# Rebuilt expert routing: last output product by column halves, router straight into tokens by experts, earlier normalising, shorter softmax

## The chip, the core and the metric

The kernel runs on one core of a Trainium2 chip. Its engines are TensorE (PE, matrix products; its weight loads are listed apart as PEld), VectorE (DVE), ScalarE (ACT), GpSimd (POOL) and SyncE (SP), which here only issues DMA transfers. Each engine works through a queue of its own in program order; semaphores order them against each other. Products are written to PSUM, eight banks of 128 partitions by 512 float32. The metric is the device time of one execution in microseconds.

## What is computed

Two layers of a diffusion backbone over 128 prompt and 256 sample tokens of width 1024, all in float32. A layer mixes tokens (three branches, gates, one output projection), adds the result to x, normalises and runs a mixture of 16 experts in which each expert chooses its tokens. The capacity is 16 tokens of the prompt and 32 of the samples. The part that matters here, cut from the reference:

```python
def block(x, mod, lp, ctx=None):
    sh1, sc1, g1, sh2, sc2, g2 = jnp.split(mod, N_MOD, axis=-1)
    h = rmsnorm(x, lp['norm1_g']) * (1 + sc1) + sh1
    y, new = token_mixing(h, lp, ctx)
    x = x + g1 * y
    h = rmsnorm(x, lp['norm2_g']) * (1 + sc2) + sh2
    x = x + g2 * ec_moe(h, lp['w_router'], lp['w_gate'], lp['w_up'], lp['w_down'])
    return x, new

def ec_moe(h, w_router, w_gate, w_up, w_down):
    b, n, d = h.shape
    cap = CAPACITY_FACTOR * n // N_EXPERTS
    aff = jax.nn.softmax(jnp.einsum('bnd,de->ben', h, w_router).astype(jnp.float32), axis=1)
    vals, idx = lax.top_k(aff, cap)
    xg = jax.vmap(lambda hb, ib: hb[ib])(h, idx)
    ...
```

## The kernel before

**Tiles and streams.** The 384 tokens are three tiles of 128: tile 0 is the prompt, tiles 1 and 2 the samples, and they are handled in the order 1, 2, 0. Everything is written by hand: each engine's program is a list of steps, and `plan_banks` gives each step its PSUM bank and its turn in it. `wait_full` waits until a bank's product is complete, `wait_read` until it has been read.

**Weights.** They stream from HBM through a ring of eight 1 MB slots (`ring`), in the expert phase sixteen (eight more in `M`, as 2 MB pairs). SyncE issues the loads in one order; each waits until its slot's last reader is done. In a layer the expert stage is eight pairs of experts with twelve 2 MB loads each. Some of the first pair's weights are loaded during mixing. After them come the slots of the last mixing units, which wait for the output products (`wo`), the load that waits for x (`x_mixed`), and the resident weights of the last pair (`load_resident`, into `arena`, `const` and `hT`), which wait for the router of tile 0 and the gate rows. Every later load waits for a product of an expert pair: the first of them for the first half product of the first pair (`first_half_used`).

**Between mixing and experts.** `project_out(n, t, lo, hi)` is the output product of column half n (512 columns) and tile t, eight products (kb) of merged by w_out, of which a call does lo to hi. VectorE's `add_mixed(n, t)` multiplies it by the gate row and adds it to x; the first half signals `x_front`, the second `x_mixed`. TensorE's `turn_x(t, h)` transposes four 128-column blocks of x, and ScalarE or VectorE (`turned`) copies them to `hT`. The router (`router`) then multiplies: its weights `wrA` (32 columns for each block) are the stationary operand, the 128 tokens move, four blocks stand side by side in the array's column groups and leave four partial sums of experts by tokens; ScalarE copies these (`router_part`), and `route` folds and turns them into tokens by experts with one more product. VectorE's `logits` scales by rstd and adds a constant, takes the maximum, subtracts it; ScalarE takes exp; `affinities` sums, inverts and scales. The affinities are turned to experts by tokens (`turn_affinities`), `top` runs rounds of MAX8 and MATCH_REPLACE8 (four for the samples, two for the prompt), `number` numbers the chosen tokens, `turn_slots` turns them back, `slots` copies and `chosen` compares them with slot numbers into the selection `gsel`. The gathers, products of the normalised x (`xn`, by ScalarE's `normal_x`) with gsel write the first group's tokens, which ScalarE and VectorE move to `xcur` (`first_samples`, `first_prompts`). `gate_row` products (L2027) make the rows of the second gate. `merged` lies in the same memory as `xn`, as blocks by all tokens, so that normalising waits for the last output product. Then come the expert pairs (`pair_step`, L2136).

In the trace a float32 product stands as two passes, so `x8` in the program's order is `x16` in the trace; transposes are single.

Of the kernel before, what the change touches and what calls it, by code (L numbers as in the profile page):

```python
# [12 lines left out]
P = 128  # L13
# [30 lines left out]
_sizes = [("ident", P), ("fold", NE), ("slotno", 2 * SLOTS),  # L44
# [11 lines left out]
def const_table():  # L56
# [13 lines left out]
    put("fold", (r[:, None] % 32 == np.arange(NE)[None, :]))  # L70
# [47 lines left out]
def plan_banks(l):  # L118
# [62 lines left out]
    for name, b in ((("wo", 0, 1), 5), (("wo", 1, 1), 6), (("wo", 0, 2), 7), (("xt", 1, 0), 0), (("xt", 1, 1), 1),  # L181
                    (("wo", 1, 2), 5), (("rpart", 1), 2), (("xt", 2, 0), 0), (("route", 1), 3), (("wo", 0, 0), 6),
                    (("xt", 2, 1), 1), (("rpart", 2), 2), (("route", 2), 3), (("wo", 1, 0), 7), (("afft", 0), 4),
                    (("xt", 0, 0), 5), (("slt", 0), 4), (("modb", 10, 0), 6), (("xt", 0, 1), 5), (("modb", 11, 0), 7),
                    (("rpart", 0), 4), (("route", 0), 5), (("afft", 1), 5), (("slt", 1), 5)):
        use(name, b)
# [78 lines left out]
def hybrid_step(nc, a, outs):  # L265
    with ExitStack() as ctx:
# [10 lines left out]
        merged = xn[:, :, :].rearrange("p t d -> p (t d)").rearrange("p (k n) -> p k n", n=TOK)  # L277
# [82 lines left out]
        rpart = arena[:, 1792:2048].rearrange("p (a b) -> p a b", b=P)  # L360
# [22 lines left out]
        fold = cst_("fold")  # L383
# [60 lines left out]
        x_front = sem("x_front")  # L444
        wshift_ready = sem("wshift_ready")
# [87 lines left out]
        def _(sp):  # L533
# [47 lines left out]
            def load_resident(l):  # L581
# [68 lines left out]
        def _(pool):  # L650
# [11 lines left out]
            for l in range(L):  # L662
# [57 lines left out]
                wait_full(pool, l, ("rpart", TILES[-1]))  # L720
# [23 lines left out]
        def _(act):  # L744
# [84 lines left out]
            for l in range(L):  # L829
# [146 lines left out]
                def router_part(t):  # L976

                    ps = wait_full(act, l, ("rpart", t))
                    read(l, ("rpart", t), F(rpart[:, t % 2, :], ps[:, 0:P], ACT.Copy))
# [6 lines left out]
                def normal_x(t):  # L986

                    act.wait_ge(rstd_ready, NPOW * (l + 1) - T + TURN[t] + 1)
                    F(xn[:, t, :], x[:, t, :], ACT.Copy, scale=rstd[:, 95 + t:96 + t]).then_inc(xn2_ready, 1)

                square_x(1)
                turned(1, 0)
                router_part(1)
# [3 lines left out]
                router_part(2)  # L997
                expert_exp(2)
                act.wait_ge(xss_ready, xs[0])
                turned(0, 0)  # L1000
                wait_full(act, l, ("wo", 1, 0))
                normal_x(1)
                square_x(0)
                turned(0, 1)
                router_part(0)
                normal_x(2)
                expert_exp(0)
                normal_x(0)
                for i in (10, 11):
                    ps = wait_full(act, l, ("modb", i, 0))  # L1010
                    if i == 10:
                        wait_full(act, l, ("modb", 11, 0))
                    read(l, ("modb", i, 0), F(g2slot[:, (i - 10) * 512:(i - 9) * 512], ps[:, :], ACT.Copy))
# [51 lines left out]
                first_samples(0)  # L1065
                first_samples(2)
                first_prompts(0)
# [5 lines left out]
        def _(dve):  # L1073
# [92 lines left out]
            def merge(l, b, j):  # L1166
# [3 lines left out]
                dst = merged[:, j, :] if b == 0 else gated  # L1170
                V.scalar_tensor_tensor(dst, tanh_g[:, j % 2, :], 1.0, ps[:, 0:TOK], ALU.add, ALU.mult)\
                    .then_inc(bank_read[turn(l, ("br", b, j))[0]], 1)
                wait_read(dve, l, ("br", b, j))
                if b:
                    V.tensor_tensor(merged[:, j, :], merged[:, j, :], gated, ALU.add).then_inc(merged_ready, 1)
# [1120 lines left out]
```

## Time and profile before

| what | us |
|---|---|
| median of 3 runs (lowest, highest) | 1750.67 (1750.56, 1751.0) |
| the profiled execution, its span | 1750.49, 1748.5 |
| TensorE busy, of the span | 1674.4 (96%) |
| VectorE, ScalarE, GpSimd busy | 659.4, 310.2, 118.7 |
| DMA mean over the span | 306 GB/s |
| output products start, layer 0 and 1 | 381.3, 1247.2 |
| first expert pair starts, layer 0 and 1 | 439.8, 1305.65 |

The rows further on give times in microseconds from the start of the span. A chain of work is read from its end back: each piece is what released the next one or stood ahead of it on its engine. "issue" in it is time in which nothing that the profile shows was waited for. The granted TensorE clock was 1.0 over the whole span, that is 2.4 GHz.

### The profile page before, as it was taken

The page shows a single profiled execution, that of the slowest core. Times are in us where ns is not written, and L with a number is a line of the kernel's source. Part 1 is how long each engine was busy: PE and PEld are TensorE (multiplying, and loading weights), DVE is VectorE, ACT ScalarE, POOL GpSimd, SP SyncE. Part 2 cuts the span into 40 slices and gives each one's busy share as a digit, 9 for nine tenths or more (in the row PEclk, how much of TensorE's full clock was granted, in tenths as well). Part 3 has the DMA queues.
Part 4 walks back from the last instruction along what each step waited for, and adds up shares of the span by engine and source line. Part 5 has one row for each costly group of instructions (what it writes and reads, how often), then busy time and mean ns, then how long its engine had stood idle before and what let it go on. Part 6 is the DMA issues. An engine that isn't in the chain of part 4 may idle for free.

```text
span 1748.5 us, 18810 instructions
## 1 busy us (share of the span) xinstructions
PE 1674.4 (96%) x7072; PEld 782.8 (45%) x7072; DVE 659.4 (38%) x1394; ACT 310.2 (18%) x792; POOL 118.7 (7%) x161
## 2 busy tenths in 40 slices
PE   7999999999999998898999999999999999988988
PEld 3456566554333232242345566665553433323322
DVE  2257666676112120121124566666651111211211
ACT  2234322032001010000022432222130100000100
POOL 0251000000000000000012500000000000000000
PEclk9999999999999999999999999999999999999999
DMA  9531333766999999999983223338669999999997
GB/s 395 191 123 36 134 121 133 294 253 265 383 427 428 427 430 427 430 427 428 426 358 144 103 84 137 117 118 340 258 229 418 426 429 426 430 427 430 428 428 318
DMA packets 51123, 534.33 MB, mean 306 GB/s; under 512 B 6065, under 2 KB 7249, under 8 KB 11377
## 3 DMA queue, kind: packets, MB, share of 16 engines
q1 hardware_dynamic: 47232, 523.27, 72.7%
q0 software_dynamic: 2112, 7.97, 1.3%
q10 hardware_dynamic: 1712, 2.20, 0.4%
q8 instruction: 42, 0.69, 0.2%
q14 instruction: 25, 0.20, 0.0%
HBM read 531.29 MB, written 2.13 MB: 305 GB/s over the span
## 4 chain that ended last, share of the span: by engine, by line
PE 79%; DMA 20%; DVE 1%; issue 0%; POOL 0%; ACT 0%; SPq 0%; DVEq 0%
PE bank L2136 24%; DMA ring<-in_w_moe 18%; PE bank L1722 14%; PE bank L1741 7%; PE bank L1788 6%; PE bank L2173 5%; PE bank L1973 5%; PE bank L1825 2%; DMA ring<-in_w_mix 2%; PE bank L1885 2%; PE bank L2040 1%; PE bank L1750 1%; PE bank L1860 1%; PE bank L1765 1%; PE bank L1710 1%; PE bank L1713 1%
## 5 line engine op out<-in xcount | busy, mean ns | idle before, releaser
L1722 PE MATMUL bank<-hT,ring 128*128 128x384 f32 x768 | 257.7, 489 | 0.0
L2136 PE MATMUL bank<-M,hT 128*64 128x512 f32 x1024 | 227.9, 595 | 16.1 <-DMA M<-in_w_moe 16.1
L2136 PE MATMUL bank<-ring,hT 128*64 128x512 f32 x976 | 220.1, 594 | 9.9 <-DMA ring<-in_w_moe 9.9
L1722 PEld LDWEIGHTS bank<-hT,ring 128*128 128x128 f32 x768 | 142.9, 190 | 99.8 <-issue 8.1
L2136 PEld LDWEIGHTS bank<-M,hT 128*64 128x64 f32 x1024 | 71.6, 137 | 162.7 <-issue 135.0
L2136 PEld LDWEIGHTS bank<-ring,hT 128*64 128x64 f32 x976 | 70.0, 137 | 146.8 <-issue 130.5
L1741 PE MATMUL bank<-M,ring 128*128 128x384 f32 x384 | 132.1, 487 | 0.0
L2136 PE MATMUL bank<-M 128*64 128x512 f32 x512 | 115.4, 595 | 12.9 <-DMA M<-in_w_moe 12.9
L2136 PE MATMUL bank<-ring,M 128*64 128x512 f32 x512 | 115.3, 596 | 12.3 <-DMA ring<-in_w_moe 10.9
L1033 ACT ACTIVATE M<-bank 128x512 f32<-128x512 f32 x32 | 19.1, 598 | 568.2 <-PE bank L2136 568.2
L1788 PE MATMUL bank<-ring,hT 128*128 128x512 f32 (+1 forms) x288 | 117.3, 567 | 1.6 <-DVE hT L1158 1.1
L1602 DVE SCALAR_TENSOR_TENSOR M<-M,bank 128x512 f32<-128x512 f32 x32 | 22.0, 688 | 226.9 <-ACT M L1033 226.9
L1607 DVE SCALAR_TENSOR_TENSOR M<-M,bank 128x512 f32<-128x512 f32 x32 | 22.0, 688 | 209.8 <-PE bank L2136 209.8
L1615 DVE TENSOR_TENSOR M<-bank,g2slot 128x512 f32<-128x512 f32 x32 | 22.1, 692 | 204.0 <-PE bank L2136 204.0
L2173 PE MATMUL bank<-M 128*128 128x512 f32 x192 | 93.7, 622 | 2.5 <-DVE M L1615 2.5
L1741 PEld LDWEIGHTS bank<-M,ring 128*128 128x128 f32 x384 | 71.4, 190 | 47.4 <-ACT M L827 1.1
L1973 PE MATMUL bank<-ring,xn 128*128 128x512 f32 x192 | 86.0, 596 | 0.0
L1403 DVE SCALAR_TENSOR_TENSOR g2slot<-ring,cs,g2slot 128x512 f32<-128x512 f32 x120 | 81.9, 746 | 1.4 <-DVE g2slot L1403 0.4
L1788 PEld LDWEIGHTS bank<-ring,hT 128*128 128x128 f32 x288 | 54.2, 190 | 62.5 <-issue 60.6
L1403 DVE SCALAR_TENSOR_TENSOR arena<-ring,cs,arena 128x512 f32<-128x512 f32 x120 | 81.5, 746 | 0.3
L1626 DVE TENSOR_TENSOR x<-x,bank 128x512 f32<-128x512 f32 x96 | 66.0, 687 | 31.4 <-PE bank L2173 31.4
L2136 PEld LDWEIGHTS bank<-M 128*64 128x64 f32 x512 | 37.0, 137 | 83.9 <-issue 75.4
(249 smaller groups left out, 1547.3 us busy)
## 6 DMA issues: line engine op xcount, KB each, us to landing
ring<-in_w_moe SPq DMA_DIRECT2D x92, 2048.0 KB, 28.6
M<-in_w_moe SPq DMA_DIRECT2D x90, 2048.0 KB, 29.2
ring<-in_w_mix SPq DMA_DIRECT2D x110, 1024.0 KB, 4.9
M<-in_w_moe SPq DMA_DIRECT2D x12, 1024.0 KB, 10.0
arena<-in_w_moe SPq DMA_DIRECT2D x4, 1024.0 KB, 11.7
ring<-in_w_mix SPq DMA_DIRECT2D x4, 576.0 KB, 5.0
arena<-in_bias_rows POOLq DMA_DIRECT2D x4, 512.0 KB, 5.8
g2slot<-in_bias_rows POOLq DMA_DIRECT2D x4, 512.0 KB, 7.3
```

The costliest lines, as they stand in the source:

```text
L1403: ins = V.scalar_tensor_tensor(acc, w[:, q, :], cs[:, kb, s:s + 1], acc, ALU.mult, ALU.add)
L1602: V.scalar_tensor_tensor(th[:, h, :], th[:, h, :], 1.0, bank[b][:, :], ALU.add, ALU.mult)\
L1615: V.tensor_tensor(osb[:, n * 512:(n + 1) * 512], bank[b][:, :], g2slot[:, n * 512:(n + 1) * 512], ALU.mult).then_inc(bank_read[b], 1)
L1626: V.tensor_tensor(xs, xs, bank[b][:, :], ALU.add).then_inc(bank_read[b], 1)
L1722: ins = mm(ps[:, 0:TOK], w[:, q, (j % 4) * P:(j % 4 + 1) * P], hT[:, 4 * h + q, :], start=(h == 0 and q == 0), stop=(h == 1 and q == 3))
L1741: ins = mm(ps[:, 0:TOK], w[:, q, (j % 4) * P:(j % 4 + 1) * P], y[:, q, :], start=(q == 0), stop=(q == 3))
L1788: ins = mm(ps[:, 0:n], hT[:, 4 * h + q, t * P:(t + 1) * P], w[:, q, 0:n], start=(h == 0 and q == 0), stop=(h == 1 and q == 3))
L1825: ins = mm(ps[:, 0:TOK], w[:, q, g * P:(g + 1) * P], hT[:, 4 * h + q, :], start=(h == 0 and q == 0), stop=(h == 1 and q == 3))
L1885: ins = mm(ps[:, :], ckvT[:, k, t * P:(t + 1) * P], w[:, k, h * 512:(h + 1) * 512], start=(k == 0), stop=(k == 1))
L1973: ins = mm(ps[:, :], merged[:, kb, t * P:(t + 1) * P], w[:, kb % 4, :], start=(kb == 0), stop=(kb == 7))
L2136: ins = mm(bank[b][64 * e:64 * e + 64, :], lhs(e, 4 * h + q), w, start=(h == 0 and q == 0), stop=(h == 1 and q == 3))
L2173: mm(bank[b][:, :], selT[:, t * P:(t + 1) * P], osb[:, n * 512:(n + 1) * 512], start=True, stop=True).then_inc(bank_full[b], 1)
```

## The change

It rewrites the stretch between the output products and the first expert pair, in seven places.

- `merged` is stored by tiles, so that each tile's part can be overwritten when its own products are done; `normal_x(1)` and `normal_x(2)` come earlier on ScalarE.
- The router keeps the token block of `hT` (128 columns) as the stationary operand and moves `wrA` (16 columns), which gives tokens by experts at once: `rpart`, `route`, `fold` and ScalarE's copy go. A tile's router is eight products in two calls of four.
- The last output product, of tile 0's second 512 columns, is made as two products of 256 columns (`project_half`), with adds (`add_half`) and turns (`turn_quarter`, `turned_quarter`) of their own; ScalarE squares x(0) in two parts.
- The router's weights are negated, so that the minimum of the negated logits serves ScalarE's exp as its bias, with the sum taken by ScalarE's accumulator.
- VectorE does `top` and `number` of the samples ahead of `add_mixed(0, 0)`.
- The prompt's selection is compared straight out of PSUM over 16 slots of four experts (`chosen_prompt`); GpSimd zeroes the rest once.
- The order of gathers, gate rows and turns on TensorE is another, and `load_resident` also waits for the last rstd.

The diff, cut to its core:

```diff
-        merged = xn[:, :, :].rearrange("p t d -> p (t d)").rearrange("p (k n) -> p k n", n=TOK)
+        merged = xn[:, :, :].rearrange("p t (k c) -> p t k c", c=P)
...
                 wait_full(sp, l, ("modb", 11, 0))
+                sp.wait_ge(rstd_ready, NPOW * (l + 1))
...
+                pool.wait_ge(merged_ready, 24 * (l + 1))
+                nc.gpsimd.memset(gsel[:, 0, :], 0.0).then_inc(gsel_zero, 1)
...
                 def expert_exp(t):
 
                     act.wait_ge(exp_in_ready, 3 * l + TURN[t] + 1)
-                    F(aff[:, t, :], logit[:, t, :], ACT.Exp).then_inc(exp_ready, 1)
+                    F(aff[:, t, :], logit[:, t, :], ACT.Exp, scale=-1.0, bias=small[:, t, 0:1], accum_out=small[:, t, 1:2])\
+                        .then_inc(exp_ready, 1)
...
+                def add_half(h):
+
+                    name = ("wo", 1, 0) if h else ("wo_first", 0)
+                    ps = wait_full(dve, l, name)
+                    lo, hi = 512 + 256 * h, 768 + 256 * h
+                    step(V.tensor_tensor(ps[:, 0:256], ps[:, 0:256], g1b[:, 0, lo:hi], ALU.mult))
+                    V.tensor_tensor(x[:, 0, lo:hi], x[:, 0, lo:hi], ps[:, 0:256], ALU.add).then_inc(x_mixed if h else x_quarter, 1)
...
-                                           ALU.mult, ALU.add).then_inc(bank_read[b], 1)
+                                           ALU.mult, ALU.subtract).then_inc(bank_read[b], 1)
                     dve.wait_ge(bank_read[b], n + 1)
-                    step(V.reduce_max(small[:, t, 0:1], logit[:, t, :], axis=AX))
-                    V.tensor_scalar(logit[:, t, :], logit[:, t, :], small[:, t, 0:1], None, ALU.subtract)\
-                        .then_inc(exp_in_ready, 1)
+                    V.tensor_reduce(small[:, t, 0:1], logit[:, t, :], AX, ALU.min).then_inc(exp_in_ready, 1)
...
-                    step(V.reduce_sum(small[:, t, 1:2], aff[:, t, :], axis=AX))
                     step(V.reciprocal(small[:, t, 2:3], small[:, t, 1:2]))
...
+                def chosen_prompt():
...
+                    V.tensor_tensor(gsel[:, 0, :].rearrange("p (e s) -> p e s", s=SLOTS)[:, :, 0:CP],
+                                    ps[:, 0:4].unsqueeze(2).to_broadcast([P, 4, CP]),
+                                    slotno[:, 0, 0:CP].unsqueeze(1).to_broadcast([P, 4, CP]),
+                                    ALU.is_equal).then_inc(gsel_ready, 1)
...
-                add_mixed(0, 0)
                 top(0, P, TOK, (0, 1, 2, 3))
                 number(2 * P)
-                add_mixed(1, 0)
+                add_mixed(0, 0)
                 slots(0, 1, T)
                 chosen(0, (1, 2))
+                add_half(0)
+                add_half(1)
+                turned_quarter(0)
+                turned_quarter(1)
                 x_variance(0)
...
+                def project_half(h, lo, hi):
...
+                        ins = mm(ps[:, 0:256], merged[:, 0, kb, :], w[:, kb % 4, h * 256:(h + 1) * 256],
+                                 start=(kb == 0), stop=(kb == 7))
...
-                def router(t):
-
-                    for h in range(2):
-                        wait_read(pe, l, ("xt", t, h))
-                    ps = begin(l, ("rpart", t))
-                    for kb in range(KB):
-                        c = 32 * (kb % 4)
-                        ins = mm(ps[c:c + 32, 0:P], wrA[:, min(t, 1), kb, :], hT[:, kb, t * P:(t + 1) * P],
-                                 start=(kb < 4), stop=(kb >= 4))
-                    done(l, ("rpart", t), ins)
...
+                def router(t, h):
...
+                    for kb in range(4 * h, 4 * h + 4):
+                        ins = mm(ps[:, 0:NE], hT[:, kb, t * P:(t + 1) * P], wrA[:, min(t, 1), kb, 0:NE],
+                                 start=(kb == 0), stop=(kb == 7))
```

TensorE around tile 0's last output product, before (L1973 the output products, L2012 the turn of the affinities, L1987 a turn of x, L2020 the turn of the slot numbers, L2027 a gate row):

```order
L2012 MATMUL bank4<-const,M 16x128 x2
L1973 MATMUL bank7<-ring,xn 128x512 x3
L1987 MATMUL bank5<-const,x 128x128 x4
L1973 MATMUL bank7<-ring,xn 128x512 x3
L2020 MATMUL bank4<-const,M 128x16 x2
```

and after (L2017 the output products, L2078 the turn of the affinities, L2031 the half products, L2086 the turn of the slot numbers, L2058 the turn of x):

```order
L2078 MATMUL bank4<-const,M 16x128 x2
L2017 MATMUL bank6<-ring,xn 128x512 x3
L2031 MATMUL bank7<-ring,xn 128x256 x4
L2031 MATMUL bank2<-ring,xn 128x256 x4
L2086 MATMUL bank4<-const,M 128x16 x2
L2058 MATMUL bank5<-const,x 128x128 x4
L2031 MATMUL bank7<-ring,xn 128x256 x4
L2031 MATMUL bank2<-ring,xn 128x256 x4
```

The turn of the slot numbers now stands ahead of half of the last output products, which are eight products of 256 columns there.

TensorE from the router of tile 0 to the first pair, before (L1997 the router, L2005 the fold, L2040 gathers of the samples, L2098 of the prompt):

```order
L1997 MATMUL bank4<-hT,arena 32x128 x8
L2005 MATMUL bank5<-const,arena 128x16
L2027 MATMUL bank7<-g2slot,const 128x512
L2040 MATMUL bank0<-M,xn 128x4x32 x4
L2012 MATMUL bank5<-const,M 16x128
L2040 MATMUL bank1<-M,xn 128x4x32 x4
L2040 MATMUL bank2<-M,xn 128x4x32 x4
L2020 MATMUL bank5<-const,M 128x16
L2040 MATMUL bank3<-M,xn 128x4x32 x4
L2098 MATMUL bank4<-M,xn 128x64 x2
```

and after (L2068 the router, L2093 gate rows, L2102 gathers of the samples, L2127 of the prompt):

```order
L2068 MATMUL bank4<-arena,hT 128x16 x4
L2093 MATMUL bank6<-arena,const 128x512
L2068 MATMUL bank4<-arena,hT 128x16 x4
L2102 MATMUL bank1<-M,xn 128x4x32 x4
L2078 MATMUL bank5<-const,M 16x128
L2093 MATMUL bank6<-arena,const 128x512
L2093 MATMUL bank7<-g2slot,const 128x512 x2
L2086 MATMUL bank5<-const,M 128x16
L2127 MATMUL bank4<-M,xn 128x64 x2
L2127 MATMUL bank5<-M,xn 128x64 x2
L2102 MATMUL bank2<-M,xn 128x4x32 x4
L2102 MATMUL bank3<-M,xn 128x4x32 x4
```

Three gate rows moved behind the turn of the prompt's affinities, and the gathers into banks 2 and 3 behind the turn of its slot numbers (L2086) and two of its gathers.

VectorE at the same place, before (L1510 ends the numbering of the samples, L1454 and L1456 are an add to x, L1515 the slot copy):

```order
L1510 TENSOR_TENSOR M<-M 16x256
L1454 TENSOR_TENSOR bank7<-bank7,M 128x512
L1456 TENSOR_TENSOR x<-x,bank7 128x512
L1515 COPY M<-bank4 128x32
L1522 TENSOR_TENSOR M<-M,const 128x256 x2
```

and after (L1543 ends the numbering, L1466 and L1468 the add of the first 512 columns, L1480 and L1481 the two adds of 256):

```order
L1543 TENSOR_TENSOR M<-M 16x256
L1466 TENSOR_TENSOR bank6<-bank6,M 128x512
L1468 TENSOR_TENSOR x<-x,bank6 128x512
L1548 COPY M<-bank4 128x32
L1564 TENSOR_TENSOR M<-M,const 128x256 x2
L1480 TENSOR_TENSOR bank7<-bank7,M 128x256
L1481 TENSOR_TENSOR x<-x,bank7 128x256
```

The add that stood ahead of the top-8 rounds, into bank 6, now stands behind the numbering.

## Rows read from the trace of the kernel before

**Rows 1.** The page, part 4: the chain that ended last, by engine.

```profile
PE 79%; DMA 20%; DVE 1%; issue 0%; POOL 0%; ACT 0%; SPq 0%; DVEq 0%
```

**Rows 2.** Chain of the whole run: start us, length us, what.

```profile
439.81 20.75 PE bank L2136 x96
...
557.00 26.09 DMA ring<-in_w_moe
...
818.13 3.65 PE bank L2136 x16
```

**Rows 3.** Windows: span, busy us of each engine (count), clock, DMA share, GB/s.

```profile
430.00:440.00 10.00, 8.79 (x74) 7.05 (x74) 5.41 (x22) 6.68 (x15) 2.06 (x4) 1.00 0.98 405
440.00:450.00 10.00, 10.00 (x48) 3.30 (x46) 1.62 (x5) 0.70 (x2) 0.00 (x0) 1.00 0.72 229
450.00:460.00 10.00, 10.00 (x50) 3.30 (x46) 0.69 (x1) 0.00 (x0) 0.00 (x0) 1.00 1.02 437
```

**Rows 4.** Issues of SyncE queue, 427 to 460: start us, length us, transfer.

```profile
427.22 0.33 SPq L559 DMA_DIRECT2D ring<-in_w_moe  x1
...
433.36 0.43 SPq L588 DMA_DIRECT2D hT<-in_w_moe  x1
443.44 0.33 SPq L572 DMA_DIRECT2D M<-in_w_moe  x1
```

**Rows 5.** Chain of work, 376 to 446: start us, length us, what.

```profile
406.48 0.57 PE bank L1997 x16
...
411.08 0.13 PE bank L2005 x2
...
421.32 0.22 PE bank L2012 x2
...
424.55 2.58 PE bank L1973 x6
...
431.21 0.29 ACT arena L979
431.49 0.14 issue
...
436.70 0.20 PE bank L2020
436.91 1.09 PE bank L2040 x8
437.99 1.82 PE bank L2098 x16
```

**Rows 6.** The page, part 5: weight loads of gate products, mean ns.

```profile
L1722 PEld LDWEIGHTS bank<-hT,ring 128*128 128x128 f32 x768 | 142.9, 190 | 99.8 <-issue 8.1
```

**Rows 7.** Timeline of VectorE, 421 to 440: start us, us, operation [idle before].

```profile
421.57 0.42 DVE L1498 MAX8 M<-bank 16x8 f32<-16x256 f32 x1 [0.51 <-PE bank L2012]
...
426.45 0.41 DVE L1510 TENSOR_TENSOR M<-M 16x256 f32<-16x256 f32 x1
427.17 0.70 DVE L1454 TENSOR_TENSOR bank<-bank,M 128x512 f32<-128x512 f32 x1 [0.30 <-PE bank L1973]
427.90 0.69 DVE L1456 TENSOR_TENSOR x<-x,bank 128x512 f32<-128x512 f32 x1
...
432.11 0.23 DVE L1479 SCALAR_TENSOR_TENSOR M<-bank,rstd,rcon 128x16 f32<-128x16 f32 x1 [2.15 <-PE bank L2005]
...
432.58 0.23 DVE L1483 TENSOR_SCALAR M<-M 128x16 f32<-128x16 f32 x1
...
437.31 0.43 DVE L1522 TENSOR_TENSOR M<-M,const 128x256 f32<-128x256 f32 x1
```

**Rows 8.** VectorE's groups of line and shape: busy us, mean ns.

```profile
L1340 DVE TENSOR_TENSOR M<-bank,rstd 128x256 f32<-128x256 f32 x16 | 6.8, 424 | 0.3
...
L1570 DVE TENSOR_SCALAR hT<-bank,amp,shift 128x64 f32<-128x64 f32 x8 | 2.4, 338 | 2.4 <-PE bank L2098 2.4
```

**Rows 9.** Timeline of ScalarE, 427 to 435.

```profile
429.59 0.19 ACT L966 ACTIVATION_READ_ACCUMULATOR hT<-x 128x1 f32 x1
```

More of the change, by code:

```diff
@@ L1174, in merge @@
                 if b:
[L1175 removed]
+                    V.tensor_tensor(merged[:, :, j, :], merged[:, :, j, :], tiles(gated), ALU.add).then_inc(merged_ready, 1)
                 else:
@@ L1977, in project_out, with turn_quarter @@
                             done(l, ("wo", n, t), ins)
+                def project_half(h, lo, hi):
+                    name = ("wo", 1, 0) if h else ("wo_first", 0)
+                    ps = begin(l, name) if lo == 0 else bank[turn(l, name)[0]]
+                    for kb in range(lo, hi):
+                        if kb % 4 == 0:
+                            arrived(l, ("wo", 1, kb // 4))
+                        w = unit_view(("wo", 1, kb // 4))
+                        ins = mm(ps[:, 0:256], merged[:, 0, kb, :], w[:, kb % 4, h * 256:(h + 1) * 256],
+                                 start=(kb == 0), stop=(kb == 7))
+                        if kb == 3 and h:
+                            ins.then_inc(first_half_used, 1)
+                        if kb == 7:
+                            done(l, name, ins)
+                def turn_quarter(h):
+                    ps = begin(l, ("xt", 0, 1 + h))
+                    if h:
+                        pe.wait_ge(x_mixed, 3 * (l + 1))
+                    else:
+                        pe.wait_ge(x_quarter, l + 1)
+                    for k in range(2):
+                        c = 512 + 256 * h + k * P
+                        ins = turn_over(ps[:, k * P:(k + 1) * P], x[:, 0, c:c + P], ident)
+                    done(l, ("xt", 0, 1 + h), ins)
                 def turn_x(t, h):
@@ L2029, in gate_row, with sample, gather_sample @@
                         done(l, ("modb", i, 0), ins)
-                def gather_sample(gr, bs, first=False):
+                def sample(b, i):
+                    kb = 2 * b + i
+                    v = bank[b][:, i * 256:(i + 1) * 256].rearrange("p (e s) -> p e s", s=SLOTS)
+                    for t in (1, 2):
+                        ins = mm(v[:, :, CP:USED], xn[:, t, kb * P:(kb + 1) * P],
+                                 gsel[:, t, :].rearrange("p (e s) -> p e s", s=SLOTS)[:, :, CP:USED],
+                                 start=(t == 1), stop=(t == 2))
+                    return ins
+                def gather_sample(gr, bs):
                     pe.wait_ge(gsel_ready, 3 * (l * NG + gr) + 2)
@@ L2036, in gather_sample, with first_sample, prompt @@
                         for i in range(2):
[L2037 to L2044 removed]
+                            sample(b, i)
+                def first_sample(b, i):
+                    if i == 0:
+                        pe.wait_ge(bank_read[b], in_pair(l, b, 0, 0, 0))
+                        sample(b, i)
+                    else:
+                        sample(b, i).then_inc(bank_full[b], 1)
+                def prompt(b):
+                    ps = begin(l, ("prompt", b))
+                    for i in range(2):
+                        ins = mm(ps[:, i * 64:(i + 1) * 64].rearrange("p (e s) -> p e s", s=CP), xn[:, 0, (2 * b + i) * P:(2 * b + i + 1) * P],
+                                 gsel[:, 0, :].rearrange("p (e s) -> p e s", s=SLOTS)[:, :, 0:CP], start=True, stop=True)
+                    done(l, ("prompt", b), ins)
                 def gather_prompt(gr):
@@ L2102, in pair_step @@
+                prompt(2)
+                prompt(3)
                 def pair_step(gr, c, more, last=False, first=False):
```

163 lines of the change are left out of this document (90 added, 73 removed).

## The prediction, made before the changed kernel was run

> **What bounds the kernel now.** I read the page's chain of work first, then the chain of the whole run in order of time, then the windows around the first expert pair, the issues of SyncE's DMA queue, and last the chain and the VectorE rows of the stretch that the change rewrites. The page puts 79% of the span on TensorE and 20% on DMA [rows 1]. In order of time those DMA parts are not spread out: from the start of the experts at 439.81 TensorE runs alone, at 557.00 it waits 26.09 us for weights, and from there to 818.13 it waits for weights again and again [rows 2]. So the expert phase ends when the weight stream ends, and the question is what starts that stream. The windows show it: in 440 to 450 the DMA engines are 0.72 busy and move 229 GB/s, from 450 they are full [rows 3]. SyncE's issues say why: the load of 443.44 waits for the first half product of the first pair, 3.6 us after the pair's start at 439.81 [rows 2, 4], and each load behind it for a later one. All that was issued before them (five loads of together 5 MB, the first at 427.22, the last at 433.36 [rows 4]) is in by about 442, since 428 GB/s take 12.3 us for it and it started at about 429. Hence the stream runs full from about 449 and **moves one for one with the start of the first pair**, both ways: a pair that starts later by s delays the end of that layer's experts by s. An earlier start would be passed on up to about 4 us, where the 5 MB of earlier loads would still fill the engines. The tail of the layer (818.13 on) and the next mixing stage hang on that end. The layers run the same program over the same sizes, the second one's experts 865.8 us after the first's, so the change in time is 2 x s. The quantity to work out is one: how far the first pair's start, 439.81, moves. In the stretch before it (402 to 440) the chain is nearly all TensorE [rows 5], so TensorE's own work counts there, not only hand-offs.
>
> **The change part by part**, in layer 0, per layer.
>
> (1) *Router of tiles 1 and 2.* Before, 16 small passes with 32-column weights took 0.57 us (0.036 each) and the fold product 0.13 us, 0.70 in all [rows 5]; the copy by ScalarE between them lay beside the output products. After, the 8 products of a tile keep the token block (128 columns) as weights and move 16 columns. A float32 product is two passes in the trace, so these are 16 passes, each with a 128x128 weight load of its own. The nearest rows are the gathers, also 128x128 weights with a new load each: 8 passes with 128 moving columns in 1.09 us, 16 with 64 moving columns in 1.82 us [rows 5]. Halving the columns has not shortened the pass, so the weight load sets it, 0.114 us; I take that. The ends are 0.036 (the old router) and 0.190 (the weight load's own duration where a long product hides it [rows 6]). 16 x 0.114 = 1.82, so +1.12 a tile, **+2.24** for two. It lies between output products in an ordered queue on TensorE; nothing hides it.
>
> The Trainium skill speaks against this part too: its page "TensorE: Matmul & The Clock Gate", section "LDWEIGHTS (loading the stationary operand)", gives columns/1.2 ns, an estimate of 107 ns for 128 columns and 27 ns for 32. The gathers' 114 ns and the old router's 36 ns agree with it within 10 ns. The same page's section "Back-to-back issue gap" gives about 81 ns a matmul at 128 columns in a stream; by that the three routers would cost 1.6 us less a layer and the time would be some 3 us lower than forecast. The gathers' row speaks against it here.
>
> (2) *The turn of the samples' slot numbers and the wait for tile 0.* The turn (0.22) moves from behind the last output product to ahead of it: **+0.22** there. In the same place VectorE now does the top-8 rounds and the numbering ahead of tile 0's first residual add, and TensorE's turn of x(0) waits for that add. VectorE's path from the turn of the affinities: 0.25 to the first MAX8 at 421.57, 5.29 to the end of the numbering (426.45 + 0.41), 0.06 + 1.42 for the add, 0.14 to TensorE: 7.16 [rows 5, 7]. TensorE's: 0.22 for the turn, six passes of 0.43 (2.58 [rows 5]), two half products of 1.72, 0.22: 6.46. **+0.70** of wait, with the last output products queued behind it. If the half products were slower, the wait would shrink by as much: 0 to 1.1.
>
> (3) *Column halves.* Four half sets of 8 passes at 256 columns: half of 0.43 is 0.215, well above the 0.114 of a weight load, so the sum stays 6.88 us; bounds 0 to +0.8. What is gained is the last add: two operations of 0.42 on 256 columns [rows 8] instead of 0.70 and 0.69 [rows 7]: **-0.50**. SyncE's load behind that product (427.22 before) is later by (1) and (2), 3.2 us, and with it the 5 MB; this keeps its distance to the first pair.
>
> (4) *From the finished x(0) to its logits*: before 428.59 to 432.11, 3.52 us [rows 7]. After: 0.14 to TensorE, a turn of two blocks 0.22, half the router 0.91, a gate row 0.86 (two passes of 0.43), the second half 0.91, and 0.3 to VectorE: 3.35; the removed copy (0.29 and 0.14 of hand-off [rows 5]) and fold are paid back by weight loads. **-0.15**. The square of tile 0 is in two parts and its rstd ready before that; the half squares and x's quarter copies lie beside these products, and would cost their 0.4 if they did not.
>
> (5) *Shorter softmax*: the subtraction and the sum on VectorE go, 0.20 of the chain each (the first is the one at 432.58 [rows 7]); ScalarE adds the read of its accumulator, 0.19 of which half overlapped at 429.59 [rows 9]. **-0.31**; ends -0.4 and -0.2. The top-8 rounds and numbering of tile 0 follow unchanged.
>
> (6) *Chosen prompt tokens.* From the end of the slot turn (436.91) to the first prompt gather (437.99 in the chain, issued 0.15 earlier) lay VectorE's evacuation of a gather, a copy and a compare of 0.43 over 256 columns [rows 5, 7]. Now there is one compare over 64 out of PSUM, 0.34 by the nearest row [rows 8], and VectorE is free. **-0.46** (0.94 to 0.48).
>
> (7) *Order of the gathers.* Two of the four sample gathers (16 passes) now stand between the prompt gathers, behind the last wait, where before 8 of the last 16 overlapped the slot copy and the others a wait: 16 x 0.114 = **+1.82**. Their evacuation by ScalarE and VectorE has 1 to 3 us until the pair's first products need it.
>
> *Nothing*: the negated router weights and the strided merge are the same operations on as many elements; normalising tiles 1 and 2 moves to ScalarE's gap before the last product and was 1.1 to 1.2 us beside other work; the new wait on rstd in SyncE's queue is long met; the memset on GpSimd stands in an idle stretch; the prompt copies of the gate rows come 1 us ahead of their bank's next use (if late, they would hold two prompt gathers, up to 0.5).
>
> Sum: 2.24 + 0.22 + 0.70 - 0.50 - 0.15 - 0.31 - 0.46 + 1.82 = **3.56 us later per layer**, first pair at about 443.4, and 7.1 us for two. The profiled execution took 1750.49 us (span 1748.5), the median of the runs is 1750.67, so no correction: 1750.5 + 7.1 = **1757.6 us**. Own range, with load spacing 0.111 to 0.125, the wait 0 to 1.1, half products +0.8 and a gather copy +0.5: s from 2.7 to 5.5, 1755.9 to 1761.5.
>
> **Rivals.** *A, the router's passes are as short as the old ones* (16 moving columns, weight loads hidden): 0.078 x 48 = 3.7 us less per layer, s = -0.2, **1750.1**: not slower. Speaks for it: the fold with 16 columns took 0.13 for two passes only. Against: that row has 0.065 a pass at best with one of its two loads already hidden under a long product, and the gathers show 0.114 in a stream. It decides where the spacing falls below about 0.05. *B, the stream does not follow the first pair*: if earlier loads fed it past 449, a later start would vanish in the wait at 557.00: **1750.5**. Against it: the 229 GB/s at 440 to 450 [rows 3]. *C, hand-offs bound the tail*: TensorE is busy 8.79 us of 430 to 440 [rows 3]; with A's spacing (0.13 less a tile) and these 1.2 us of idling all filled, s = -1.6, **1747.3** (1745 to 1749.5). Needs A and no wait in (2) at all. *D, the small passes take the load's full 0.190*: 0.076 x 48 = 3.6 us more per layer, **1764.9**. Against it again the gathers.
>
> **How the numbers follow.** Forecast 0.70; A 0.09; B 0.05; C 0.11, of which 0.07 beyond 0.2%; D 0.05. 0.2% (3.5 us) is about what a measurement of this kernel can tell from no change. Slower: 0.70 + 0.05 = 0.75; same: 0.09 + 0.05 + 0.04 = 0.18; faster: 0.07. The range takes in A and B and the forecast's own range: 1749.5 to 1761.5, which leaves out D, most of C and a little of the forecast.
>
> **What would show it.** The 16 router passes of a tile in about 1.8 us (A: 0.6; D: 3.0); the last output product ending 3.2 us later (430.3); a wait of about 0.7 ahead of the turn of x(0); the logits of tile 0 at about 434.6; the first pair at about 443.4; two sample gathers of 1.8 us between the slot compare and it; DMA full from about 452.5; the wait at 557 no shorter and 3.6 us later; the second layer's experts 7 us later. The prediction is wrong if the first pair starts within 1 us of 439.81, or if it starts later and the waits for weights shrink instead.

## The result, and the profile after

The changed kernel takes 1756.3 us (median of 8 runs, 1755.75 to 1756.63) against 1750.53 us for the kernel before, run beside it (8 runs, 1750.19 to 1751.0): ratio 1.0032, interval 1.0023 to 1.0042. It is **5.8 us slower**. The prediction was 1757.6 us, range 1749.5 to 1761.5, slower with 0.75. The range was drawn wide enough to hold two rivals that say "not slower"; the forecast's own range was 1755.9 to 1761.5, and the result lies near its lower end.

The chain of the whole run in order of time (start us, length us, what), the lines that answer to [rows 2]:

```profile
442.90 20.75 PE bank L2226 x96
...
560.09 26.26 DMA ring<-in_w_moe
...
821.39 3.65 PE bank L2226 x16
```

The first expert pair starts at 442.90 instead of 439.81, TensorE's first long wait for weights at 560.09 instead of 557.00, and the product behind the last of them at 821.39 instead of 818.13. The wait itself is as long as before (26.3 us). Part of this has nothing to do with the change: the output products start at 381.77 here and at 381.49 before (by the chain; the 381.3 and 1247.2 of the table ahead of the prediction are the same starts read from TensorE's timeline, which sets them some 0.17 us sooner), and in the other profiles of this study, some of them of kernels that are unchanged up to that point, between 381.1 and 382.1. So I measure the **stretch** from the start of the output products (the piece of 48 passes that takes 20.68 us) to the start of the first pair: 439.81 - 381.49 = 58.32 us before, 442.90 - 381.77 = 61.13 after; in the second layer 58.32 before (1305.65 - 1247.33) and 61.19 after (1311.78 - 1250.59). That is 2.81 and 2.87 us more, 5.7 together, which is the result. The windows over the first layer's stretch, before and after, split it into TensorE's work and its waits (columns as in [rows 3]):

```profile
381.49:439.81 58.32, 57.12 (x239) 29.67 (x240) 40.87 (x96) 13.98 (x29) 3.62 (x6) 1.00 0.74 294
381.77:442.90 61.13, 59.55 (x249) 36.23 (x250) 40.47 (x93) 14.24 (x32) 3.94 (x7) 1.00 0.72 278
```

TensorE is busy 59.55 us instead of 57.12 and idle 1.58 instead of 1.20: of the 2.81 us, 2.43 are more work and 0.38 more waiting.

Windows (span, busy us of PE, PEld, DVE, ACT and POOL with counts, granted clock, DMA share, GB/s) and SyncE's issues, answering to [rows 3, 4]:

```profile
440.00:450.00 10.00, 10.00 (x60) 5.26 (x61) 1.92 (x6) 2.63 (x8) 0.11 (x1) 1.00 0.76 272
450.00:460.00 10.00, 10.00 (x48) 3.30 (x46) 1.38 (x2) 0.56 (x1) 0.00 (x0) 1.00 0.97 382
```

```profile
430.16 0.33 SPq L559 DMA_DIRECT2D ring<-in_w_moe  x1
...
436.92 0.33 SPq L585 DMA_DIRECT2D arena<-in_w_moe  x1
...
438.96 0.42 SPq L589 DMA_DIRECT2D hT<-in_w_moe  x1
446.52 0.33 SPq L572 DMA_DIRECT2D M<-in_w_moe  x1
```

The DMA engines have their gap as before, 0.76 busy at 440 to 450; it reaches past 450 now. The first load that waits for an expert product goes out at 446.52 instead of 443.44, again 3.6 us behind the pair's start. Of the five earlier loads the first goes out 2.9 us later than before, as the prediction had it, but the resident weights follow 4.9 us later (436.92, before 432.02) and 5.6 us later (438.96, before 433.36): they wait for the gate rows, three of which the change moved back. That these 5 MB would keep their distance to the first pair was wrong for 2 MB of them; the long wait at 560.09 moved with the pair all the same, so nothing shows that it cost time.

The chain between 376 and 450, answering to [rows 5] (L2068 the router, L2086 the turn of the slot numbers, L2058 the turn of x, L2078 that of the affinities, L2102 the gathers of the samples, L2127 of the prompt):

```profile
406.76 1.69 PE bank L2068 x16
...
414.61 0.80 PE bank L2068 x8
...
416.36 0.80 PE bank L2068 x8
...
425.99 0.63 PE bank L2058 x4
...
430.07 0.44 PE bank L2102 x4
...
431.55 0.80 PE bank L2068 x8
...
435.70 0.27 PE bank L2078
...
438.55 0.19 PE bank L2086
...
439.14 1.08 PE bank L2127 x8
440.22 1.84 PE bank L2102 x16
```

and one row of TensorE's timeline (the turn of x(0), with TensorE's idle time ahead of it and what ended it) and three of VectorE's (L1481 the last add to x(0), L1515 its logits, L1556 the prompt's compare), answering to [rows 7, 8]:

```profile
425.99 0.63 PE L2058 MATMUL bank<-const,x 128*128 128x128 f32 x4 [0.54 <-DVE x L1468]
...
430.57 0.42 DVE L1481 TENSOR_TENSOR x<-x,bank 128x256 f32<-128x256 f32 x1
...
434.21 0.23 DVE L1515 SCALAR_TENSOR_TENSOR M<-bank,rstd,rcon 128x16 f32<-128x16 f32 x1 [2.14 <-PE bank L2068]
...
438.82 0.23 DVE L1556 TENSOR_TENSOR M<-bank,const 128x64 f32<-128x64 f32 x1 [0.44 <-PE bank L2086]
```

A tile's router takes 1.69 us, or 0.80 twice, where it took 0.57 and 0.13. The turn of x(0) starts at 425.99 after a wait of 0.54 for VectorE's add. The last output product ends at 430.07, x(0) is complete at 430.99, the logits start at 434.21, the slot turn stands at 438.55, the compare of 64 columns takes 0.23, and between the prompt gathers stand 1.84 us of sample gathers.

### The profile page after: what moved, and what is told of

Its sections match the earlier page's. It is cut to its first block, busy times and chain, and to the rows that moved or that the text cites. A ratio compares the mean times of both kernels' runs of the same rounds, so it can differ in the third digit from the quotient of the medians.

```text
span 1754.4 us, 18857 instructions
## 1 busy us (share of the span) xinstructions
PE 1680.1 (96%) x7092; PEld 796.1 (45%) x7092; DVE 657.6 (37%) x1386; ACT 311.1 (18%) x798; POOL 119.4 (7%) x163
## 4 chain that ended last, share of the span: by engine, by line
PE 80%; DMA 18%; DVE 1%; issue 0%; ACT 0%; POOL 0%; SPq 0%; DVEq 0%; ACTq 0%
PE bank L2226 24%; DMA ring<-in_w_moe 18%; PE bank L1766 14%; PE bank L1785 7%; PE bank L1832 7%; PE bank L2263 5%; PE bank L2017 4%; PE bank L1869 2%; PE bank L1929 2%; PE bank L2102 2%; PE bank L1794 1%; PE bank L1904 1%; PE bank L1809 1%; PE bank L1754 1%; PE bank L1757 1%; PE bank L1718 1%
## 5 line engine op out<-in xcount | busy, mean ns | idle before, releaser
L2226 PEld LDWEIGHTS bank<-ring,M 128*64 128x64 f32 x512 | 35.8, 137 | 84.4 <-issue 71.3
```

What stands on the lines that cost most here:

```text
L2226: ins = mm(bank[b][64 * e:64 * e + 64, :], lhs(e, 4 * h + q), w, start=(h == 0 and q == 0), stop=(h == 1 and q == 3))
```

## The experiments

The times of the kernel before beside them: 1750.38 us (29 runs) for the first four, 1750.37 (25 runs) for the next four. For each kernel the stretch of the two layers is given too; it repeats within 0.1 us where nothing in it changed and shows more than the total does.

### Does the stream follow the first pair? (e7)

Only the start of the first pair was moved, in the kernel before:

```diff
-                    for i in range(2):
+                    for i in [0] * 4 + [0, 1]:
                         ins = mm(ps[:, i * 64:(i + 1) * 64]..., xn[:, 0, (2 * b + i) * P:(2 * b + i + 1) * P], gsel[:, 0, :]...,
                                  start=True, stop=True)
```

> The kernel before with each prompt gather's first product made four times more (32 passes of 128-column weights and 64 moving columns per layer, same result), so that only the start of the first pair moves. At 0.114 us a pass that is 3.65 us per layer. Theory (the weight stream follows the first pair one for one): 1757.7. Rival B of the prediction (the stream doesn't follow): 1750.5.

1757.86 us (1757.13 to 1758.15), ratio 1.0042, interval 1.0029 to 1.0056. The stretches are 61.89 us in both layers, 3.57 more than before, and the time 7.5 us more than 1750.37: 2 x 3.57 = 7.1, one for one within the scatter. The chain of the whole run:

```profile
443.31 20.75 PE bank L2136 x96
...
560.50 26.47 DMA ring<-in_w_moe
...
788.30 33.63 DMA ring<-in_w_moe
```

The pair starts 3.50 us later than in [rows 2], the first wait for weights comes 3.50 later, and the last wait begins 3.84 later (784.46 before). Nothing of the delay is absorbed on the way; rival B is out.

### The router alone, and the router undone (e1, e2)

e1 is the kernel before with this and what goes with it (no `rpart`, no `route`, no copy):

```diff
-                    ps = begin(l, ("rpart", t))
+                    ps = begin(l, ("route", t))
                     for kb in range(KB):
-                        c = 32 * (kb % 4)
-                        ins = mm(ps[c:c + 32, 0:P], wrA[:, min(t, 1), kb, :], hT[:, kb, t * P:(t + 1) * P],
-                                 start=(kb < 4), stop=(kb >= 4))
+                        ins = mm(ps[:, 0:NE], hT[:, kb, t * P:(t + 1) * P], wrA[:, min(t, 1), kb, 0:NE],
+                                 start=(kb == 0), stop=(kb == 7))
```

> The kernel before with the new router alone (tokens by experts, 16 passes a tile with 128-column weight loads; no copy, no fold). Theory (TensorE's own work sets the stretch, a pass costs its weight load, 0.100 us as measured in the changed kernel): 1.6 against 0.70 us for each of tiles 1 and 2, so the last output product ends 1.8 us later; tile 0 gets its logits 0.4 us sooner after x(0) because the copy and the fold go; the first pair starts 1.4 us later per layer, the time is 1753.4. Rival (the router is hidden, the order of the gathers is what costs): 1750.5 within 0.5.

1754.39 us (1754.03 to 1755.1), ratio 1.0022, interval 1.0013 to 1.0031; stretches 60.36 and 60.35 us, **2.0 more than before**. The part by itself costs 4.0 us where 2.9 was expected (1753.4 against 1750.5). Its routers in the chain:

```profile
406.65 1.69 PE bank L1993 x16
...
416.21 1.69 PE bank L1993 x16
...
432.40 1.80 PE bank L1993 x16
```

The three routers take 5.2 us of TensorE instead of 2.4 (0.70 twice, and 0.62 and 0.37 for tile 0), 2.8 more, and 2.0 of them reach the end. I had expected the hand-offs that go to leave tile 0 ahead by 0.4 us; the wait for the copy that stood there was 0.45 us [rows 5], its router takes 0.8 us more, and no more than 0.8 is won back in all.

e2 is the changed kernel with the old form back, its calls placed so:

```diff
-                router(1, 0)
-                router(1, 1)
+                router(1)
                 turn_x(2, 0)
                 project_out(1, 2, 4, 8)
+                route(1)
                 project_out(0, 0, 0, 2)
                 turn_x(2, 1)
-                router(2, 0)
                 project_out(0, 0, 2, 3)
-                router(2, 1)
-                project_out(0, 0, 3, 5)
+                router(2)
+                project_out(0, 0, 3, 4)
+                route(2)
+                project_out(0, 0, 4, 6)
                 turn_affinities(0, 1, T)
-                project_out(0, 0, 5, 8)
+                project_out(0, 0, 6, 8)
...
-                router(0, 0)
                 gate_row(10, 0)
-                router(0, 1)
+                router(0)
                 first_sample(1, 0)
+                route(0)
```

> The changed kernel with the router form of before (32-column weights, partial sums, copy, fold), all else as changed; the turn of the affinities comes after six of tile 0's first eight products. Theory: TensorE has 2.0 us less to do for tiles 1 and 2, but about 1.0 of it is lost to a longer wait for x(0)'s first half, since VectorE's 7.2 us from the affinities to that add then is the longer path; tail 0.3 shorter; 1.3 us per layer, 1753.7. Rival (router form indifferent): 1756.3.

1754.85 us (1753.71 to 1755.66), ratio 1.0024, interval 1.0015 to 1.0034; stretches 60.10 and 60.39, so 1.0 and 0.8 us less than the changed kernel has, where 1.3 was expected. The router work that goes is 2.7 us per layer; more than half of it comes back, first as a wait for x(0):

```profile
424.71 0.70 DVE x L1479
...
425.54 0.63 PE bank L2069 x4
426.17 3.46 PE bank L2042 x16
```

VectorE's second half of the add ends at 425.41 and the turn of x(0) follows it, as in the changed kernel, though TensorE's own work before it was 1.9 us less. TensorE now waits 1.07 us there instead of 0.54, 0.30 for VectorE's numbering instead of nothing, and 1.06 instead of 0.61 for the prompt's affinities. **So the router alone and the router undone give 4.0 and 1.5 us** (4.1 and 1.8 by the stretches). The parts don't add up: in e1 2.0 of 2.8 us of added work reach the end, and in e2, where VectorE does the top-8 rounds ahead of the add to x(0), more than half of the work that goes is replaced by waits for VectorE.

### The turn of x(0) (e8)

```diff
-                turn_x(0, 0)
                 project_half(0, 4, 8)
+                turn_x(0, 0)
                 project_half(1, 4, 8)
```

> The changed kernel with the turn of x(0)'s first 512 columns behind one more half product instead of ahead of it. Theory: TensorE's wait of 0.5 to 0.6 us for that add is covered, the last output product ends as much sooner, 1.1 us for two layers: 1755.2. Rival (the wait is covered elsewhere): 1756.3.

1754.91 us (1754.73 to 1755.27), ratio 1.0026, interval 1.0016 to 1.0036: 1.4 us less than the changed kernel where 1.1 was expected; stretches 60.60 and 60.66, 0.53 us less each, which is the 1.1.

```profile
425.28 0.22 PE bank L2086 x2
425.50 1.93 PE bank L2031 x8
427.43 0.44 PE bank L2058 x4
```

The half product follows the slot turn at once and the turn of x(0) comes behind it without a wait. So term (2) of the prediction, a wait of 0.7, was there, with 0.53 (0.54 in the timeline of the changed kernel).

### The order of the gathers (e3, e5)

```diff
                 first_sample(1, 0)
                 first_sample(1, 1)
+                first_sample(2, 0)
+                first_sample(2, 1)
                 turn_affinities(1, 0, 1)
...
                 turn_slots(1, 0, 1)
+                first_sample(3, 0)
+                first_sample(3, 1)
                 pe.wait_ge(xn2_ready, 3 * l + 3)
                 pe.wait_ge(gsel_ready, 3 * (l * NG + 1))
                 prompt(0)
                 prompt(1)
-                for b in (2, 3):
-                    for i in range(2):
-                        first_sample(b, i)
                 prompt(2)
```

> The changed kernel with the third sample gather moved ahead of the turn of the prompt's affinities and the fourth ahead of the prompt gathers, into the two waits of 0.6 and 0.4 us that TensorE has there. Theory (what counts is TensorE's total work plus its waits, not what stands behind the last wait): the waits are filled, 1.0 us per layer, 1754.3. Rival (the working of the prediction: 1.8 us less behind the last wait): 1752.6.

1755.08 us (1754.77 to 1755.81), ratio 1.0027, interval 1.0016 to 1.0037; stretches 60.72 and 60.79, 0.4 us less each: neither 1.0 nor 1.8. The end of the chain shows where the rest is:

```profile
439.65 0.41 PE bank L2127 x4
...
440.08 0.71 ACT hT L1061 x2
...
440.90 0.61 ACT g2slot L999
...
441.55 0.66 PE bank L2127 x4
442.21 7.87 PE bank L2227 x35
```

L2127 are the prompt gathers. The third of them waits for its bank, which ScalarE's copy of a gate row (L999) frees, and this copy stands behind the prompt tokens of the first gather (L1061): 1.5 us from the end of the first gather, in the first 0.45 of which the second one runs. In the changed kernel the samples' gathers ran in that time. e5 moves the copies:

```diff
                 first_samples(1)
+                first_samples(2)
                 wait_full(act, l, ("modb", 11, 0))
                 gate_copy(10)
-                first_prompts(0)
                 gate_copy(11)
-                first_samples(2)
+                first_prompts(0)
                 first_prompts(2)
```

> e3 with ScalarE's two copies of the gate rows both made ahead of its first prompt tokens. In e3 TensorE waited 1.5 us for the copy that frees the bank of the third prompt gather, so the waits that e3 filled came back behind it. Theory (TensorE's work plus waits): this wait goes, the first pair starts 1.4 us sooner than in e3 in each layer, 1752.3. Rival (ScalarE's copies only move the wait to the first pair, which then waits for the prompt tokens): 1755.1 as e3.

1753.52 us (1753.14 to 1754.11), ratio 1.0018, interval 1.0009 to 1.0027; stretches 59.90 and 59.97.

```profile
438.13 0.18 PE bank L2086
438.30 1.09 PE bank L2102 x8
439.39 1.73 PE bank L2127 x16
441.12 4.01 PE bank L2227 x17
```

The wait is gone and 1.2 us per layer are won in all by the order of the gathers, about what TensorE had waited in the changed kernel (it is busy 14.96 of the 16 us from 427 to 443 there). The 1.8 of term (7) can't be won back by moving the gathers: they cost their time wherever they stand, and only where they fill a wait are they free. The expectation (1752.3) took the chain's 1.5 us for a wait of TensorE; with the second gather inside it, 0.8 came free (60.72 to 59.90).

### Old router, waits filled: can the rest of the change win? (e4, e6)

e4 has the edits of e2, e3 and e8 together.

> e2 and e3 together, and the turn of x(0)'s first half moved behind one more half product, so that TensorE does not wait for it. Theory: last output product ends about 427.2 as in the kernel before, x(0) complete 0.5 sooner, logits 0.8 sooner, both waits filled: first pair at 438.4 against 439.8 before, 1.4 us earlier per layer; the weight stream follows it: 1747.7. Rival (the weight stream cannot start sooner): 1750.5.

1751.96 us (1751.3 to 1752.37), ratio 1.0008, interval 0.9999 to 1.0017; stretches 58.52 and 58.81. Not faster than the kernel before: the 1747.7 expected is missed by 4.3 us. The same piece through ScalarE stands in it:

```profile
437.20 0.41 PE bank L2143 x4
...
438.44 0.61 ACT g2slot L1007
...
439.10 0.66 PE bank L2143 x4
439.75 10.44 PE bank L2244 x47
```

(L2143 are the prompt gathers, L1007 is the copy, L2244 the first pair.) e6 takes it away as e5 does, and puts the normalising of tile 1 behind the exp of tile 2, for which tile 2's exp had waited:

```diff
                 router_part(2)
-                normal_x(1)
                 expert_exp(2)
+                normal_x(1)
                 normal_x(2)
```

> e4 with ScalarE's copies of the gate rows first as in e5, and with the normalising of tile 1 behind the exp of tile 2. Theory: the 1.5 us wait of e4 goes in both layers and the 0.4 us wait of the second layer too; first pair at 438.3 against 439.8 in the kernel before, 1.5 us earlier per layer, and the weight stream passes it on: 1748.6, faster than the kernel before by 1.9. Rival (an earlier start isn't passed on, since the stream is bound by the loads ahead of it): 1750.4 at best.

1749.62 us (1748.66 to 1750.52), ratio 0.9996, interval 0.9987 to 1.0005; stretches 57.70 and 58.00, that is 0.62 and 0.32 us less than before, where 1.5 was expected. From e4 to e6 0.8 us are won in each layer, again the 1.5 less the second gather. The move of the normalising brought nothing that shows: the second layer wins no more than the first, and its affinities are turned 36.57 us behind the start of its output products in both kernels (1283.97 in e4, 1283.40 in e6). The sum against before, 0.94, fits the 0.75 in the time, but the interval of the time includes no change. The traces say a little more: the last wait for weights ends 0.50 us sooner than before in the first layer (817.59, before 818.09) and 0.88 sooner in the second (1683.02, before 1683.90), with pairs that start 0.80 and 0.82 sooner. So an earlier start seems to be passed on too, in one profile and for less than 1 us. In the chain and in the window:

```profile
437.28 1.73 PE bank L2143 x16
439.01 11.30 PE bank L2244 x51
```

```profile
430.00:440.00 10.00, 9.83 (x73) 7.00 (x74) 4.90 (x21) 6.28 (x16) 1.93 (x4) 1.00 0.96 404
```

TensorE is busy 9.83 of 10 us where it was 8.79 before [rows 3]. Over the whole stretch it waits 0.47 us (0.30 for the numbering and 0.17 for the affinities) where it waited 1.20 before, and it is busy 57.23 us where it was 57.12. So little is left to fill, and the rest of the change has taken no work from TensorE.

### The softmax alone, and what sets a router pass (e9, e10)

e9 is the kernel before with the negated weights, the minimum as bias and the accumulated sum, one profiled run:

> The kernel before with the shorter softmax alone (negated router weights, minimum as bias, sum by ScalarE's accumulator). The prediction's working gave this 0.31 us per layer. Theory (TensorE's work plus waits): before tile 0's affinities are turned, TensorE waits only 0.04 us for them, since gathers fill the time, so the stretch from the output products to the first pair shortens by 0.05 us per layer and not by 0.3: 58.27 against 58.32 us, time 1750.4.

Time 1750.01 beside 1750.23 (one run each; the stretches carry the reading), stretches 58.12 and 58.12: 0.20 us less each, between the 0.05 expected here and the 0.31 of the prediction's term (5).

```profile
432.58 0.89 PE bank L2038 x8
433.47 0.12 PE bank L2010
...
433.62 0.30 DVE M L1496
```

(L2038 sample gathers, L2010 the turn of the affinities, L1496 the first MAX8.) In the kernel before, TensorE waited 0.04 us for the affinities and the turn then took 0.27. Now it stands in the stream behind the gathers and adds 0.12 plus 0.02. So the top-8 rounds start 0.15 us behind the gathers (433.62 against 433.47) instead of 0.35 (434.19 against 433.84), which is the 0.20. That a product that doesn't have to be waited for costs half as much was missing in my expectation.

e10 is the changed kernel with 64 moving columns instead of 16 in seven of a tile's eight router products, one profiled run:

```diff
-                        ins = mm(ps[:, 0:NE], hT[:, kb, t * P:(t + 1) * P], wrA[:, min(t, 1), kb, 0:NE],
+                        n = 2 if kb < 7 else 1
+                        ins = mm(ps[:, 0:32 * n], hT[:, kb, t * P:(t + 1) * P],
+                                 wrA[:, min(t, 1), kb:kb + n, :].rearrange("p a b -> p (a b)"),
                                  start=(kb == 0), stop=(kb == 7))
```

> The changed kernel with 64 moving columns in seven of the eight router products of a tile instead of 16; the first 16 hold the same logits, the rest is not read. If the weight load sets a pass, a tile's 16 passes stay at 1.6 to 1.7 us and the time at 1756.3. If the moving columns matter between 16 and 64, the pass goes from 0.100 to the 0.108 to 0.114 us of the prompt gathers, 0.5 us more for the three tiles of a layer, 1757.3.

Time 1756.08, stretches 61.15 and 61.22, as in the changed kernel (61.13, 61.19).

```profile
406.27 1.71 PE bank L2069 x16
...
414.11 0.84 PE bank L2069 x8
...
415.87 0.81 PE bank L2069 x8
```

16 passes take 1.71 instead of 1.69, 8 take 0.81 to 0.84 instead of 0.80. The three tiles together take 5.02 us instead of 4.90, 2.4% for four times the moving columns, and the products that stand between the halves of two of these routers take 0.91 instead of 0.95 each, so that the stretch grows by 0.02 and 0.03 only. The moving columns don't set the price of 0.100 to 0.107 us a pass. Nor does a pass as such, since the old router's take 0.036 with twice the columns of e10 moving. What differs between the two forms is the weights: 128 columns, or 32 in four column groups side by side. No run separates the narrower load from the side-by-side groups; the trace gives 109 ns for one load of the old form and 192 for one of the new, so loads overlap in both.

## Why the prediction was right, point by point

Step by step, in the first layer, with the 0.28 us by which that profile started late taken off the first row:

| step | predicted us | measured us |
|---|---|---|
| (1) and (2): last output product later | +3.16 | +2.66 (430.07 - 427.13 - 0.28) |
| (3) column halves: product to complete x(0) | -0.50 | -0.54 (0.92 instead of 1.46) |
| (4) complete x(0) to logits | -0.15 | -0.30 (3.22 instead of 3.52) |
| (5) logits to the turn of the affinities | -0.31 | -0.28 (1.49 instead of 1.77) |
| from there to the slot turn | 0 | +0.03 |
| (6) slot turn to the first prompt gather | -0.46 | -0.55 (0.59 instead of 1.14) |
| (7) gathers to the first pair | +1.82 | +1.79 (3.76 instead of 1.97) |
| sum | +3.56 | +2.81 |

- **What bounds the kernel** held: the weight stream moves with the first pair, one for one (e7). Rival B is refuted.
- **Term (1) was mis-sized.** I took 0.114 us a pass from the prompt gathers [rows 5]; the router's passes take 0.106 in one row of 16 and 0.100 in rows of 8, so a tile costs 0.9 to 1.0 more and not 1.12. e10 shows that the difference is not the number of moving columns; the gathers' price depends on where they stand (the same 16 take 1.73 in e5, 0.108 each, and 1.82 before); why was not looked into. Two tiles of it make 0.35 of the 0.75 us by which the sum was too high, and tile 0's share of it the 0.15 of step (4).
- **The wait in (2)** was predicted as 0.70 and is 0.54 in the trace and 0.53 by e8.
- **(3), (5), (6), (7)** hold within 0.1 us as durations on the path of the changed kernel. As causes two of them don't stand alone: (7) read as "1.8 us to be had" is refuted (0.4 in e3, 1.2 in e5), and (5) gives 0.20 alone in e9. The sum came out right in its direction and 0.75 us too high in 3.56; its larger errors all have one sign, so no luck of cancelling is in it. It could be that close since it followed one definite order of the instructions from end to end; its terms are places on that path and not what each edit is worth.
- **Nothing** for the prompt copies of the gate rows held in the changed kernel and only there: the sample gathers between the prompt gathers cover ScalarE's copy. Moved away, they expose a wait of 0.8 us (e3, e4).
- **Rival A** (short passes) is refuted by 1.69 and 0.80 in the chain and by e10; **C** with it, and e6 shows directly how little filling nearly all waits gives, 0.3 to 0.6 us per layer with the old router. **D** (3.0 us for 16 passes) is refuted by the same 1.69.

TensorE's work and waits in the first layer's stretch, from the same windows for each kernel, show which path each edit acts on (good to some 0.2 us, since the ends of products are modelled):

| kernel | stretch | busy | idle |
|---|---|---|---|
| before | 58.32 | 57.12 | 1.20 |
| e1, new router alone | 60.36 | 59.64 | 0.72 |
| changed | 61.13 | 59.55 | 1.58 |
| e2, changed with the old router | 60.10 | 57.26 | 2.84 |
| e5, changed with gathers in the waits | 59.90 | 59.35 | 0.55 |
| e6, old router, waits filled | 57.70 | 57.23 | 0.47 |

The added work is the router's: 2.5 us in e1, 2.4 in the changed kernel, and 0.1 in e2 and e6, which keep the old router. The rest of the change shows in the waits.

What the edits are worth alone: the router +4.0 us (e1). What the rest is worth with the old router depends on its order. In e4 it is +1.6 us, at the edge of the noise, of which the stretches show only 0.7 and the end of the program 1.1 in the profiled run; in e6 it is -0.75, inside the noise. The halves and the direct compare were not tried by themselves.

## What to carry to other kernels

In a stretch that one engine fills almost wholly, ask of each edit how much work it takes from or gives to that engine; a hand-off saved there is worth at most the wait that stood beside it. Swapping which operand of a small product is kept as weights can cost more than it saves: with 128 weight columns instead of 32 in four column groups, a form that saves a copy and a product cost 0.9 to 1.0 us more per tile here. Work that seems badly placed may be the cover of a wait on another engine, so follow the next bank or buffer before moving it.

## What the runs showed that I had not expected

- A small product pass with new 128x128 float32 weights costs 0.100 to 0.107 us a pass whether 16 or 64 columns move (e10), against 0.036 with 32-column weights in four column groups [rows 5].
- A transposing product that is ready when TensorE comes to it adds 0.12 us to the stream (e9), the same one after a wait 0.27 (before, 433.88). In the changed kernel a hand-off from VectorE of 0.14 stands ahead of it as well (435.57 to 435.70).
- The start of the output products, some 381 us into the span, differs by up to 1 us between the profiles (381.12 to 382.09), while the stretch behind it repeats within 0.1 us in the two layers of all kernels but e2, e4 and e6, which have the old router in the new order and take 0.3 us more in the second. What moves it was not looked into.
- e4's last expert product ends 0.5 us later than in the kernel before and its span 1.7 us later. The 1.1 us lie behind the last add, in the writing of the outputs; why is open.
